# A mixer's tail folded into the next mixer's triangular inverse, in a two-layer hybrid trunk on one core

## The chip, the cores and the metric

The kernel runs on one core of one Trainium2 chip. The metric is the device time of one launch in microseconds (us). A profile is taken by the hardware on one execution; the span is the time from its first to its last instruction.

Names used below: TensorE (PE in the rows; PEld are its weight loads), VectorE (DVE), ScalarE (ACT), and SyncE (SP), whose queue issues every load of weights here. PSUM is a tile `ps` of eight banks of 128x512 float32.

## The reference

Two decoder layers over 256 tokens and 1024 channels. Each layer runs four mixers on 256 channels each, an output projection, a cross attention over 256 memory tokens and a feed-forward block (SwiGLU in layer 0, eight experts in layer 1).

```python
for l in range(DEPTH):
    h = rmsnorm(x, norm_mix[l]); p = h @ w_in[l]
    y_a = hgrn2_mixer(...)            # first mixer
    y_b = gated_deltanet_mixer(...)   # second mixer
    y_c = rglru_mixer(...)
    y_d = rwkv7_mixer(...)            # the mixer behind the second
    x = x + concat([y_a, y_b, y_c, y_d]) @ w_out[l]
    x = x + memory_cross_attention(rmsnorm(x), mem_n, wq, wk, wv, wo)
    x = x + (swiglu(...) if l % 2 == 0 else moe_swiglu(...))
```

The second mixer (gated DeltaNet) solves a unit triangular system for each chunk of 64 tokens and then steps a state:

```python
uw = triangular_solve(I + lower, rhs)          # lower: strict part of k k^T, decayed
v_new = u - w @ state
o = (q * exp(g)) @ state + scores @ v_new
state = exp(g_last) * state + k^T v_new
```

RWKV-7 is a recurrence of the same kind, and the kernel does it in the same chunked form, with a triangular inverse of its own. Keys and values of the memory (`mem_n @ wk`, `mem_n @ wv`) depend on nothing in the layer.

## The kernel before

Every engine has a program of its own, written out by hand; semaphores join them, and each engine runs its list strictly in the order of the code. In a layer the lists run: projection `w_in`, first mixer (`hgrn`), second mixer (`deltanet`), RWKV-7 (`rwkv`), output projection (`tm_part` and `tm_product` on `w_out`), attention, feed-forward.

**The inverses.** `inverse(i)` builds the inverse of a 64x64 unit triangular matrix for 8 pairs of head and chunk, by doubling, in levels v = 0 to 6 (`LEVELS` = 7) and two groups g. Inverse 2l belongs to DeltaNet and inverse 2l+1 to RWKV-7; I call them the first and the second inverse of layer l. A level goes around three engines: TensorE makes the products `inv_t`, VectorE masks them into `T1`, TensorE makes the products `inv_p`, then VectorE adds them to `X` while ScalarE copies `Y`. Behind each level TensorE calls `after(v)` and VectorE `beside(v)`: other work, written in between. The second inverse starts when VectorE has masked a score matrix into `N` (`mask(l, 0, ...)`, semaphore `inv_n`).

**DeltaNet's tail**, between the two inverses: `solve` for the first 128 tokens, a ScalarE copy, the state product, a VectorE mask of it (`state_bd`), the product `gd_km`, a VectorE subtraction (`gd_r1`), `solve` for the last 128 tokens, a copy, `outputs`, and the head norm (`head_ss`, then a logarithm and an exponential on ScalarE in `head_rms`, then `head_out` on VectorE). Each step waits for another engine.

**Filler.** The keys and values of the memory are made in eight pieces in a layer, `kv(l, i, ks)`: piece i is one chunk of weights, and each of its eight slices k is two float32 products. TensorE does slices of them wherever it would wait. `kv` waits first for the piece's load. I write kv6 for piece 6.

**Loads.** All chunks of weights (1024 KB each) go through three buffers `raw0` to `raw2`, in the order of `plan_chunks`, from one queue (SP). Load d waits until load d-3 is used up:

```python
if d >= RAW and loads[d - RAW][0] == "kv":
    sp.wait_ge(S("kv_done"), kv_load.index(d - RAW) + 1)
elif d >= RAW:
    sp.wait_ge(S("w_lo"), load_of.index(d - RAW) + 1)
```

A chunk that is not of the memory is used up when it is split into a high and a low part: `ahead(n)` on ScalarE makes `whi` from `raw`, `ahead(n)` on VectorE makes `wlo` (semaphore `w_lo`), each up to chunk n-1. Around the change the loads are, in layer 0: w_out 0, kv4, kv5, w_out 1, kv6, w_out 2, w_out 3, kv7; in layer 1: w_out 0, kv5, w_out 1, kv6, w_out 2, w_out 3, kv7. So w_out 1 and behind it kv6 (layer 0), and kv6 itself (layer 1), wait for the low part of w_out 0. TensorE needs kv6's first slices directly behind the second inverse.

## Time and profile before

| | |
|---|---|
| median of 3 runs | 1926.84 us (1923.26 to 1929.85) |
| profiled execution, its time | 1923.63 us |
| profiled execution, its span | 1921.8 us |
| TensorE busy | 1844.5 us (96% of the span) |
| VectorE busy | 1436.4 us (75%) |
| ScalarE busy | 1153.5 us (60%) |
| mean granted TensorE clock | 0.988 of full speed |

Busy time of TensorE counts the modelled ends of pipelined matmuls. In a row of the timeline the first number is the start, the second the length, `xN` the instructions merged, and the brackets give the idle time before and who ended it. One float32 product is two instructions in these rows.

### The profile page before, as it was taken

Reading aid. Unit: us, or ns where it says so; the run is one execution under the profiler, and the core shown is the slowest. Engines: PE = TensorE matmul, PEld = TensorE weight load, DVE = VectorE, ACT = ScalarE, POOL = GpSimd, SP = SyncE. Lnnn points to the kernel's source line nnn. Section 1 sums busy time; section 2 is a strip of 40 time slices with the busy share of each in tenths; the row PEclk is TensorE's granted clock in tenths of the full one; section 3 lists DMA queues with packets and bytes.
Section 4 is the critical chain, followed back from the end, with each engine's and each line's share of the span. In section 5 each row is a group of like instructions: output and inputs, shape, how many; then the busy total and the mean of one; then the engine's idle time right before and its main releaser. Section 6 shows DMA issues by size and latency. Waiting matters only on the chain.

```text
span 1921.8 us, 30255 instructions
## 1 busy us (share of the span) xinstructions
PE 1844.5 (96%) x12776; PEld 1589.5 (83%) x12777; DVE 1436.4 (75%) x1475; ACT 1153.5 (60%) x1129; POOL 0.2 (0%) x4
## 2 busy tenths in 40 slices
PE   7999999999999988996999999999999999999996
PEld 6988789999999877895788888888888888888884
DVE  6876654544458876545889989899898998989985
ACT  6565344434344653444677777677776777767774
POOL 0000000000000000000000000000000000000000
PEclk9999999999999999998999999999999999999998
DMA  7512224455555211234799999999999999999992
GB/s 247 162 60 68 68 88 168 164 189 181 176 173 172 66 46 68 88 132 167 288 365 368 361 333 377 350 370 365 326 386 341 365 372 332 382 364 340 371 374 87
DMA packets 239452, 466.02 MB, mean 242 GB/s; under 512 B 11856, under 2 KB 87760, under 8 KB 239312
## 3 DMA queue, kind: packets, MB, share of 16 engines
q1 hardware_dynamic: 239168, 463.93, 67.6%
q8 instruction: 103, 1.69, 0.4%
q14 instruction: 37, 0.30, 0.0%
q10 hardware_dynamic: 144, 0.11, 0.0%
HBM read 462.95 MB, written 1.05 MB: 241 GB/s over the span
## 4 chain that ended last, share of the span: by engine, by line
PE 92%; DVE 6%; issue 1%; ACT 1%; DVEq 0%; DMA 0%; ACTq 0%
PE ps L2265 32%; PE ps L1696 16%; PE ps L2275 16%; PE ps L1681 15%; PE ps L1716 8%; PE ps L2321 2%; PE ps L2296 1%; PE ps L1761 1%; DVE MT L974 1%; PE ps L2336 1%; DVE TMP L974 0%; DVE MT L977 0%; DVE hT_lo L980 0%; DVE MT L1216 0%; PE ps L1786 0%
## 5 line engine op out<-in xcount | busy, mean ns | idle before, releaser
L1458 DVE TENSOR_TENSOR wlo<-raw,whi 128x2048 fp32r<-128x2048 f32 x140 | 320.5, 2291 | 55.8 <-ACT whi L843 55.6
L843 ACT ACTIVATE whi<-raw 128x2048 fp32r<-128x2048 f32 x140 | 268.9, 1922 | 120.8 <-PE ps L2275 71.3
L987 DVE TENSOR_TENSOR wlo<-raw,whi 128x2048 fp32r<-128x2048 f32 x85 | 194.5, 2289 | 83.8 <-ACT whi L494 83.7
L1458 DVE TENSOR_TENSOR wlo<-PT,whi 128x2048 fp32r<-128x2048 f32 x84 | 192.1, 2292 | 31.2 <-ACT whi L843 30.2
L494 ACT ACTIVATE whi<-raw 128x2048 fp32r<-128x2048 f32 x85 | 162.2, 1908 | 80.1 <-PE ps L1716 31.9
L2265 PE MATMUL ps<-whi,hE_hi 128*128 128x512 f32 x672 | 185.4, 398 | 2.4 <-DVE hE_lo L1527 2.4
L843 ACT ACTIVATE whi<-PT 128x2048 fp32r<-128x2048 f32 x84 | 161.4, 1922 | 34.8 <-PE ps L2265 34.2
L2265 PE MATMUL ps<-wlo,hE_hi 128*128 128x512 f32 x672 | 180.1, 390 | 0.0
L2265 PE MATMUL ps<-whi,hE_lo 128*128 128x512 f32 x672 | 179.8, 389 | 0.0
L2265 PEld LDWEIGHTS ps<-wlo,hE_hi 128*128 128x128 f32 x672 | 126.2, 188 | 27.2
L2265 PEld LDWEIGHTS ps<-whi,hE_lo 128*128 128x128 f32 x672 | 126.1, 188 | 26.7
L2265 PEld LDWEIGHTS ps<-whi,hE_hi 128*128 128x128 f32 x672 | 122.0, 188 | 24.8 <-DVE hE_lo L1527 2.6
L2275 PE MATMUL ps<-whi,act_hi 128*128 128x512 f32 x336 | 130.8, 389 | 1.4 <-DVE act_lo L1502 1.4
L2275 PE MATMUL ps<-whi,act_lo 128*128 128x512 f32 x336 | 130.8, 389 | 0.0
L2275 PE MATMUL ps<-wlo,act_hi 128*128 128x512 f32 x336 | 130.7, 389 | 0.0
L1696 PE MATMUL ps<-hT_hi,whi 128*128 128x256 f32 x848 | 120.8, 285 | 0.0
L1696 PE MATMUL ps<-hT_hi,wlo 128*128 128x256 f32 x848 | 119.0, 283 | 0.0
L1696 PE MATMUL ps<-hT_lo,whi 128*128 128x256 f32 x848 | 119.0, 283 | 0.0
L1696 PEld LDWEIGHTS ps<-hT_hi,whi 128*128 128x128 f32 x848 | 110.1, 192 | 2.3 <-issue 1.4
L1696 PEld LDWEIGHTS ps<-hT_lo,whi 128*128 128x128 f32 x848 | 109.4, 192 | 0.0
L1696 PEld LDWEIGHTS ps<-hT_hi,wlo 128*128 128x128 f32 x848 | 109.4, 192 | 0.0
L485 ACT ACTIVATE MT<-ps 128x256 f32<-128x256 f32 (+2 forms) x94 | 43.9, 467 | 104.8 <-PE ps L1696 51.6
(301 smaller groups left out, 3337.8 us busy)
## 6 DMA issues: line engine op xcount, KB each, us to landing
raw<-in_moe_w_up SPq DMA_DIRECT2D x111, 1024.0 KB, 7.1
PT<-in_moe_w_down SPq DMA_DIRECT2D x56, 1024.0 KB, 6.7
PT<-in_moe_w_gate SPq DMA_DIRECT2D x55, 1024.0 KB, 7.0
TMP<-in_moe_w_gate SPq DMA_DIRECT2D x55, 1024.0 KB, 6.9
raw<-in_moe_w_down SPq DMA_DIRECT2D x55, 1024.0 KB, 5.9
raw<-in_w_in SPq DMA_DIRECT2D x28, 1024.0 KB, 5.5
raw<-in_ffn_w_gate SPq DMA_DIRECT2D x11, 1024.0 KB, 5.4
raw<-in_ffn_w_up SPq DMA_DIRECT2D x11, 1024.0 KB, 5.5
```

The lines of the kernel that those rows point to most:

```text
L485: return chain.link(lambda: nc.scalar.activation(o, i, f, **kw))
L494: nc.scalar.activation(whi[i % SPL][:, :], raw[d % RAW][:, :], ACT.Copy).then_inc(S("w_hi"), 1)
L843: nc.scalar.activation(ex_hi[m % XSPL], ex_raw[m % XRAW], ACT.Copy).then_inc(S("w_hi"), 1)
L974: return chain.link(lambda: V.tensor_tensor(o, x0, x1, op))
L987: V.tensor_tensor(wlo[i % SPL][:, :], raw[d % RAW][:, :], whi[i % SPL][:, :].bitcast(F32), ALU.subtract).then_inc(S("w_lo"), 1)
L1458: V.tensor_tensor(ex_lo[m % XSPL], ex_raw[m % XRAW], ex_hi[m % XSPL].bitcast(F32), ALU.subtract).then_inc(S("w_lo"), 1)
L1681: return Signalled(pe.matmul(o, lhsT, rhs, start=start, stop=stop, skip_group_check=True))
L1696: ins = pe.matmul(ps[:, bank, SEQ * m:SEQ * m + SEQ], wp[a_][:, k, P * m:P * m + P], src[b_][:, k, :], start=i == 0 and k == 0, stop=last)
L1716: ins = pe.matmul(ps[:, 4 + 2 * t + hf, :], src(b_, kk, t), wp[a_][:, kk, 512 * hf:512 * hf + 512], start=first and kk == 0 and i == 0, st ...
L2265: ins = pe.matmul(ps[:, bank, :], h_[b_][:, X_K * i + k, :], wp[a_][:, k, :], start=i == 0 and n_ == 0 and k == 0, stop=i == 1 and n_ == 2 ...
L2275: ins = pe.matmul(ps[:, 4 + hf, :], act_[b_][:, P * (TM_ROWS * i + kk):P * (TM_ROWS * i + kk) + P], wp[a_][:, kk, 512 * hf:512 * hf + 512] ...
L2321: ins = pe.matmul(g_tokens(c), xs[:, t, P * c:P * c + P], oneh[:, P * t:P * t + P], start=t == 0, stop=t == 1)
```

## The change

It touches both layers. DeltaNet's tail no longer stands between the inverses; its steps stand behind the levels of the second inverse, on all three engines. For that:

- The first RWKV score product, whose mask starts the second inverse, is made in `after(6)` of the first inverse, from operands that VectorE now finishes in `beside(5)` (`B_K`). Its mask is VectorE's next work after the first inverse.
- The second inverse's `Y` of levels 0 to 4 goes to a buffer of its own, since the tail still reads the first inverse's result. DeltaNet's output is copied to the other half of that buffer (`g_out`).
- The memory pieces that lay in the tail are dealt out over the levels again; slices 6 and 7 of kv5 come behind level 6.
- On VectorE, the split of w_out 0 (`ahead(first_chunk["w_out", l] + 1)`) moves from behind level 1's mask to behind the whole second inverse, and `head_out` stands behind it.
- On ScalarE, the high part of w_out 1 moves from level 5 into the RWKV tail, before the copy of the first `solve`. A wait for `head_out` stands ahead of it.

On ScalarE:

```diff
             def rwkv(l):
+                i = 2 * l + 1
+                inverse_turned(i)
+                inverse_first(i)
+                gdn_right(l, 0)
+                inverse_level(i, 1)
+                inverse_level(i, 2)
...
+                inverse_level(i, 3)
+                gdn_right(l, 1)
+                inverse_level(i, 4)
+                act.wait_ge(S("o_full"), 2 * l + 2)
+                a(tmp(6), ps[:, 6, :], ACT.Square)
+                a(g_out(l), ps[:, 6, :], ACT.Copy).then_inc(S("o_sq"), 1)
+                inverse_level(i, 5)
+                act.wait_ge(S("rk_kb"), 2 * l + 1)
+                act.wait_ge(S("o_ss"), 2 * l + 2)
+                a(tmp(7), ps[:, 6, :], ACT.Ln, scale=1.0 / HD, bias=epsc(0))
+                a(tmp(7), tmp(7), ACT.Exp, scale=-0.5).then_inc(S("o_rn"), 1)
...
                     if t == 0:
                         act.wait_ge(S("rk_trv"), 2 * l + 2)
                         a(tmp(6), ps[:, 3, :], ACT.Copy).then_inc(S("rk_vk"), 1)
+                        act.wait_ge(S("y_put"), 4 * l + 2)
+                        ahead(first_chunk["w_out", l] + 2)
                     act.wait_ge(S("rk_u"), 2 * l + t + 1)
                     a(tmp(4)[:, 256 * t:256 * t + 256], ps[:, 7, 256 * t:256 * t + 256], ACT.Copy, scale=-1.0).then_inc(S("rk_us"), 1)
```

On VectorE (`rk_kb` and `rk_ops` say that operands are ready):

```diff
                     tt(pt(B_Q), K_KA, K_EN, ALU.mult)
+                    tt(pt(B_K), K_KK, K_EM, ALU.mult).then_inc(S("rk_kb"), 1)
...
             def rwkv(l):
                 def beside(v):
 
                     if v == 0:
-                        head_out(l, 1, ps[:, 6, :], tmp(7), lambda c: pc("gdn_norm", l), pt(B_Z), 1)
+                        tt(pt(A_I), pt(D_R), K_E, ALU.mult).then_inc(S("rk_kb"), 1)
+                        tt(cm(pt(C_X))[:, :, 0:P], cm(K_KA)[:, :, 0:P], cm(pt(A_Q))[:, :, 0:P], ALU.mult)
+                        tt(cm(pt(C_X))[:, :, P:], cm(K_KK)[:, :, P:], cm(pt(A_F))[:, :, P:], ALU.mult)
                     if v == 1:
-                        ahead(first_chunk["w_out", l] + 1)
+                        dve.wait_ge(S("state"), 3 * l + 2)
...
                     if v == 2:
                         mask(l, 1, 4, mt(1), strict).then_inc(S("rk_m"), 1)
+                        dve.wait_ge(S("gd_km"), l + 1)
+                        tt(tmp(4)[:, 256:512], tmp(4)[:, 256:512], ps[:, 6, 256:512], ALU.subtract).then_inc(S("gd_r1"), 1)
+                    if v == 3:
+                        tt(cm(pt(B_V))[:, :, 0:P], cm(pt(D_K))[:, :, 0:P], cm(pt(A_Q))[:, :, 0:P], ALU.mult)
...
                         mask(l, 2, 4, PT[:, 0:1024], incl).then_inc(S("rk_m"), 1)
+                    if v == 5:
+                        tt(K_B, pt(D_R), pt(D_K), ALU.mult)
...
+                mask(l, 0, 4, mt(3), strict).then_inc(S("inv_n"), 1)
                 inverse(2 * l + 1, after=beside)
+                ahead(first_chunk["w_out", l] + 1)
+                head_out(l, 1, g_out(l), tmp(7), lambda c: pc("gdn_norm", l), pt(B_Z), 1)
...
                 rglru(l, LEVELS)
                 chain.settle()
                 ahead(first_chunk["w_out", l] + 2)
```

On TensorE; the first piece is in the first inverse's `after`, the rest in `rwkv`, the second's:

```diff
+                    if v == LEVELS - 1:
+                        pe.wait_ge(S("rk_kb"), 2 * l + 1)
+                        scores(4, pt(B_Q), pt(B_K)).then_inc(S("rk_sc"), 1)
...
             def rwkv(l):
+                k4 = ([0, 1, 2], [3, 4], [5, 6, 7], [], [], [], [])
+                k5 = ([], [], [], [0, 1, 2], [3, 4], [5], [6, 7]) if l == 0 else ([0], [1], [2], [3], [4], [5], [6, 7])
...
+                    kv(l, 5, k5[v])
                     if v == 0:
-                        kv(l, 4 + l, [6, 7])
...
+                        pe.wait_ge(S("rk_rn"), l + 1)
+                        solve(6, 0, tmp(4)).then_inc(S("gd_u"), 1)
...
+                        pe.wait_ge(S("gd_us"), 2 * l + 1)
...
                         scores(4, pt(A_G), pt(B_K)).then_inc(S("rk_sc"), 1)
+                    if v == 2:
+                        pe.wait_ge(S("state_bd"), 3 * l + 2)
...
                     if v == 3:
+                        pe.wait_ge(S("gd_r1"), l + 1)
+                        solve(6, 1, tmp(4)).then_inc(S("gd_u"), 1)
...
                         scores(4, pt(B_Q), pt(A_I)).then_inc(S("rk_sc"), 1)
+                    if v == 4:
+                        pe.wait_ge(S("gd_us"), 2 * l + 2)
+                        outputs(6, [(tmp(6), mt(2))], tmp(3)[:, 256:512], g_qe(l)).then_inc(S("o_full"), 1)
...
+                        head_ss(l, 1, tmp(6))
                     if v == LEVELS - 1:
-                        pe.wait_ge(S("y_put"), 4 * l + 2)
+                        pe.wait_ge(S("o_rn"), 2 * (l + 1))
...
                 inverse(2 * l + 1, after=turn_operands)
                 pe.wait_ge(S("rk_m"), 3 * (l + 1))
+                pe.wait_ge(S("rk_ops"), l + 1)
                 kv(l, 6, [0, 1])
```

**Where the split of w_out 0 stands.** This is VectorE in layer 0 before the change: levels 1 and 2 of the second inverse. `wlo2<-raw0` is the low part of w_out 0; L974 writes `T1` and `X`.

```order
L974 TENSOR_TENSOR MT<-ps,con16b 128x256 [waits y_put,inv_t]
L974 TENSOR_TENSOR MT<-ps,con16b 128x256 [waits inv_t1,inv_t]
L987 TENSOR_TENSOR wlo2<-raw0,whi2 128x2048 [waits w_hi]
L974 TENSOR_TENSOR MT<-MT,ps 128x256 [waits inv_t1,inv_p]
L974 TENSOR_TENSOR MT<-MT,ps 128x256 [waits inv_xy,inv_p]
L974 TENSOR_TENSOR MT<-ps,con16b 128x256 [waits inv_xy,inv_t]
L974 TENSOR_TENSOR MT<-ps,con16b 128x256 [waits inv_t1,inv_t]
```

With the change, the same engine at levels 5 and 6 and behind them; L1311 is the inverse's last copy.

```order
L986 TENSOR_SCALAR MT<-ps 64x256 [waits inv_xy,inv_t]
L986 TENSOR_SCALAR MT<-ps 64x256 [waits inv_t1,inv_t]
L989 SCALAR_TENSOR_TENSOR MT<-ps,con 128x1024 [waits inv_t1,rk_sc]
L1311 COPY MT<-ps 64x256 [waits rk_m,inv_p]
L1311 COPY MT<-ps 64x256 [waits inv_xy,inv_p]
L996 TENSOR_TENSOR wlo2<-raw0,whi2 128x2048 [waits w_hi]
L983 TENSOR_TENSOR TMP<-spare_hi1_50,TMP 128x512 [waits inv_xy,o_rn]
L989 SCALAR_TENSOR_TENSOR TMP<-TMP,par,PT 128x256 [waits dve_step] x2
```

The split has moved past five levels, to directly behind the last copy, with `head_out` behind it.

**The loads.** SP's list in layer 0 around them, the same rows in the same order in both kernels (the line numbers are those of the kernel with the change). `raw1<-in_xattn_wv`, second of the two, is kv6; the `raw0<-in_w_out` ahead of it is w_out 1.

```order
L437 DMA raw1<-in_xattn_wv 128x8x256 [waits kv_done]
L437 DMA raw2<-in_xattn_wv 128x8x256 [waits kv_done]
L437 DMA raw0<-in_w_out 128x2x1024 [waits w_lo]
L437 DMA raw1<-in_xattn_wv 128x8x256 [waits kv_done]
L437 DMA raw2<-in_w_out 128x2x1024 [waits kv_done]
```

No row moved: w_out 1 still waits for `w_lo`, the split of w_out 0, and kv6 still stands behind it.

**TensorE between the inverses.** Layer 0 before the change, from the last products of the first inverse to the tail's state product (`raw2` is the last filler of the first inverse, `raw1` is kv4).

```order
L1681 MATMUL ps<-MT 64x64 [waits inv_t1,inv_c]
L1681 MATMUL ps<-MT 64x64 x3
L1681 MATMUL ps<-memT_55,raw2 128x256 [waits raw_in2,kv_put]
L1681 MATMUL ps<-memT_55,raw2 128x256 x3
L1681 MATMUL ps<-TMP,MT 64x64 [waits rk_rn,inv_xy]
L1681 MATMUL ps<-TMP,MT 64x64 x7
L1681 MATMUL ps<-raw1,memT_55 128x256 [waits raw_in1,kv_put]
L1681 MATMUL ps<-raw1,memT_55 128x256
L1681 MATMUL ps<-TMP 128x128 [waits gd_us]
L1681 MATMUL ps<-TMP 128x128
```

The same place with the change:

```order
L1689 MATMUL ps<-MT 64x64 [waits inv_t1,inv_c]
L1689 MATMUL ps<-MT 64x64 x3
L1689 MATMUL ps<-memT_55,raw2 128x256 [waits raw_in2,kv_put]
L1689 MATMUL ps<-memT_55,raw2 128x256 x3
L1689 MATMUL ps<-PT 128x128 [waits rk_kb]
L1689 MATMUL ps<-PT 128x128 x7
L1689 MATMUL ps<-MT,con 64x64 [waits inv_n,inv_xy]
L1689 MATMUL ps<-MT,con 64x64 x15
L1689 MATMUL ps<-con,spare_hi1_50 64x64 [waits inv_c,inv_xy]
```

The score product (`PT`, waits `rk_kb`) has come forward to the filler's end, and the second inverse's first product, which waits for `inv_n`, stands directly behind it with no filler between them.

**TensorE at the end of the second inverse**, layer 0 with the change; `raw1` is kv6, `raw2` kv5.

```order
L1689 MATMUL ps<-MT 64x64 [waits inv_t1,inv_c]
L1689 MATMUL ps<-MT 64x64 x3
L1689 MATMUL ps<-raw2,memT_55 128x256 [waits raw_in2,raw_in1]
L1689 MATMUL ps<-raw2,memT_55 128x256 x3
L1692 MATMUL ps<-con,PT 128x128 [waits o_rn]
L1692 MATMUL ps<-con,PT 128x128 x3
L1689 MATMUL ps<-raw1,memT_55 128x256 [waits rk_ops,raw_in1,rk_m,inv_xy]
L1689 MATMUL ps<-raw1,memT_55 128x256 x3
L1689 MATMUL ps<-TMP,MT 128x64 [waits rk_vk]
L1689 MATMUL ps<-TMP,MT 128x64 x3
```

Before it was the same without the two `raw2` rows: slices 6 and 7 of kv5 have come behind level 6, and kv6's first slices still follow the four transposes.

## Rows read from the trace of the kernel before

**Rows 1.** The page, part 4: the chain that ended last, by engine.

```profile
PE 92%; DVE 6%; issue 1%; ACT 1%; DVEq 0%; DMA 0%; ACTq 0%
```

**Rows 2.** Windows: length; busy PE, PEld, DVE, ACT, POOL; PEclk; DMA; GB/s.

```profile
186.20:233.70 47.50, 44.45 (x800) 36.80 (x800) 26.45 (x49) 14.91 (x26) 0.00 (x0) 1.00 0.25 82
235.30:239.00 3.70, 3.68 (x10) 2.94 (x11) 3.46 (x6) 0.29 (x1) 0.00 (x0) 0.54 0.01 2
725.70:766.20 40.50, 36.68 (x768) 31.26 (x767) 26.41 (x49) 14.91 (x26) 0.00 (x0) 1.00 0.22 80
767.90:771.40 3.50, 3.50 (x9) 2.79 (x10) 3.32 (x6) 0.00 (x0) 0.00 (x0) 0.51 0.00 0
```

**Rows 3.** Timeline of TensorE, layer 0, from the first inverse on.

```profile
184.29 1.99 PE L1681 MATMUL ps<-memT,raw 128*128 128x256 f32 x8
...
195.55 1.16 PE L1681 MATMUL ps<-PT 64*128 64x128 f32 x16
...
199.42 1.15 PE L1681 MATMUL ps<-MT,con 64*64 64x64 f32 x32
...
212.97 1.22 PE L1681 MATMUL ps<-MT 64*64 64x64 f32 x64 [0.15 <-DVE MT L974]
...
231.22 2.46 PE L1681 MATMUL ps<-MT 64*64 64x64 f32 x32
233.62 0.66 PE L1684 MATMUL ps<-con,PT 128*128 128x128 f32 x4
235.32 3.63 PE L1681 MATMUL ps<-raw,memT 128*128 128x256 f32 x8 [1.04 <-DVE MT L1301]
```

**Rows 4.** Timeline of VectorE, layer 0, same stretch.

```profile
189.04 0.42 DVE L974 TENSOR_TENSOR TMP<-ps,con 128x256 f32<-128x256 f32 x1 [4.23 <-PE ps L1681]
...
196.75 1.23 DVE L980 SCALAR_TENSOR_TENSOR MT<-ps,con 128x1024 f32<-128x1024 f32 x1 [1.19 <-PE ps L1681]
198.01 0.87 DVE L974 TENSOR_TENSOR MT<-MT,con16b 64x256 f32<-64x256 f32 x2
198.92 0.43 DVE L974 TENSOR_TENSOR MT<-ident_b,MT 128x256 f32<-128x256 f32 x1
...
206.60 2.28 DVE L987 TENSOR_TENSOR wlo<-raw,whi 128x2048 fp32r<-128x2048 f32 x1
...
234.32 0.94 DVE L1301 COPY MT<-ps 64x256 f32<-64x256 f32 x2
```

**Rows 5.** Timeline of SP's queue, layer 0: w_out 1, then kv6.

```profile
208.91 0.37 SPq L431 DMA_DIRECT2D raw<-in_w_out  x1
209.32 0.47 SPq L431 DMA_DIRECT2D raw<-in_xattn_wv  x1
```

**Rows 6.** Issues of that stretch: KB each, us from issue to landing.

```profile
raw<-in_w_out SPq DMA_DIRECT2D x1, 1024.0 KB, 4.8
raw<-in_xattn_wv SPq DMA_DIRECT2D x1, 1024.0 KB, 7.4
```

**Rows 7.** Timeline of TensorE, layer 1.

```profile
763.77 2.46 PE L1681 MATMUL ps<-MT 64*64 64x64 f32 x32
...
767.86 3.68 PE L1681 MATMUL ps<-raw,memT 128*128 128x256 f32 x8 [1.04 <-DVE MT L1301]
```

**Rows 8.** Timeline of VectorE, layer 1.

```profile
766.87 0.94 DVE L1301 COPY MT<-ps 64x256 f32<-64x256 f32 x2
```

**Rows 9.** Issue of kv6 in layer 1, at 748.37.

```profile
raw<-in_xattn_wv SPq DMA_DIRECT2D x1, 1024.0 KB, 5.2
```

**Rows 10.** Issues at 288.7 to 290, three behind each other.

```profile
raw<-in_xattn_wo SPq DMA_DIRECT2D x1, 1024.0 KB, 10.8
```

**Rows 11.** Timeline of ScalarE, layer 0.

```profile
229.48 1.91 ACT L494 ACTIVATE whi<-raw 128x2048 fp32r<-128x2048 f32 x1
...
242.39 0.38 ACT L485 ACTIVATE TMP<-ps 128x256 f32<-128x256 f32 x1 [1.45 <-PE ps L1681]
```

**Rows 12.** A window early in the span, columns as in rows 2.

```profile
26.80:31.40 4.60, 4.55 (x26) 3.02 (x27) 3.01 (x10) 0.00 (x0) 0.00 (x0) 0.63 0.87 258
```

More of the change, by code:

```diff
@@ L1276, in inverse @@
                 N, X, Y, T1 = mt(3), X_INV, mt(5), mt(0)
+                Y0 = y_work(i)
                 for v in range(LEVELS):
@@ L1368, in deltanet @@
                 inverse(2 * l, after=beside)
-                dve.wait_ge(S("state"), 3 * l + 2)
-                tt(tmp(3)[:, 256:512].rearrange("p (c n) -> p c n", c=2), ps[:, 1, 0:256].rearrange("p (c n) -> p c n", c=2),
-                   rep(bdones, 2), ALU.mult).then_inc(S("state_bd"), 1)
-                dve.wait_ge(S("gd_km"), l + 1)
-                tt(tmp(4)[:, 256:512], tmp(4)[:, 256:512], ps[:, 1, 256:512], ALU.subtract).then_inc(S("gd_r1"), 1)
-                rwkv_operands(l)
-                mask(l, 0, 2, mt(3), strict).then_inc(S("inv_n"), 1)
             def rwkv(l):
@@ L1386, in beside @@
+                    if v == 3:
+                        tt(cm(pt(B_V))[:, :, 0:P], cm(pt(D_K))[:, :, 0:P], cm(pt(A_Q))[:, :, 0:P], ALU.mult)
+                        tt(cm(pt(B_V))[:, :, P:], cm(pt(D_R))[:, :, P:], cm(pt(A_Q))[:, :, P:], ALU.mult)
                     if v == 4:
                         mask(l, 2, 4, PT[:, 0:1024], incl).then_inc(S("rk_m"), 1)
+                    if v == 5:
+                        tt(K_B, pt(D_R), pt(D_K), ALU.mult)
+                        for c in range(2):
+                            s_ = slice(256 * c, 256 * c + 256)
+                            ts(K_B[:, s_], K_B[:, s_], pc("rwkv_r_k", l, c), ALU.mult).then_inc(S("rk_ops"), 1 if c else 0)
@@ L2081, in deltanet @@
-                for c in range(2):
-                    mm(ps[:, 1, P * c:P * c + P], tmp(3)[:, P * c:P * c + P], tmp(6)[:, P * c:P * c + P]).then_inc(S("state"), 1 if c else 0)
-                kv(l, 4 + l, [1])
-                pe.wait_ge(S("state_bd"), 3 * l + 2)
-                for c in range(2):
-                    mm(ps[:, 1, 256 + P * c:256 + P * c + P], g_kbe(l)[:, 256 * c + P:256 * c + 256], tmp(3)[:, 256 + P * c:256 + P * c + P]).then_inc(S("gd_km"), 1 if c else 0)
-                kv(l, 4 + l, [2])
@@ L2088, in deltanet @@
-                pe.wait_ge(S("gd_r1"), l + 1)
-                solve(6, 1, tmp(4)).then_inc(S("gd_u"), 1)
-                kv(l, 4 + l, [3])
-                pe.wait_ge(S("gd_us"), 2 * l + 2)
-                outputs(6, [(tmp(6), mt(2))], tmp(3)[:, 256:512], g_qe(l)).then_inc(S("o_full"), 1)
-                pe.wait_ge(S("rk_kb"), l + 1)
-                scores(2, pt(B_Q), pt(B_K)).then_inc(S("rk_sc"), 1)
-                head_ss(l, 1, tmp(6))
-                kv(l, 4 + l, [4, 5])
             def rwkv(l):
+                k4 = ([0, 1, 2], [3, 4], [5, 6, 7], [], [], [], [])
@@ L2107, in turn_operands @@
                     if v == 1:
-                        pe.wait_ge(S("rk_ops"), l + 1)
-                        pe.wait_ge(S("o_rn"), 2 * (l + 1))
+                        pe.wait_ge(S("gd_us"), 2 * l + 1)
+                        for c in range(2):
+                            mm(ps[:, 6, P * c:P * c + P], tmp(3)[:, P * c:P * c + P], tmp(6)[:, P * c:P * c + P]).then_inc(S("state"), 1 if c else 0)
                         scores(4, pt(A_G), pt(B_K)).then_inc(S("rk_sc"), 1)
+                    if v == 2:
+                        pe.wait_ge(S("state_bd"), 3 * l + 2)
+                        for c in range(2):
+                            mm(ps[:, 6, 256 + P * c:256 + P * c + P], g_kbe(l)[:, 256 * c + P:256 * c + 256], tmp(3)[:, 256 + P * c:256 + P * c + P]).then_inc(S("gd_km"), 1 if c else 0)
@@ L2143, in rwkv @@
                 pe.wait_ge(S("rk_rs"), 2 * l + 1)
-                solve(7, 0, tmp(7)).then_inc(S("rk_u"), 1)
+                solve(7, 0, tmp(2)).then_inc(S("rk_u"), 1)
                 kv(l, 6, [3])
@@ L2155, in rwkv @@
                 pe.wait_ge(S("rk_rs"), 2 * l + 2)
-                solve(7, 1, tmp(7)).then_inc(S("rk_u"), 1)
+                solve(7, 1, tmp(2)).then_inc(S("rk_u"), 1)
                 kv(l, 6, [6])
```

81 lines of the change are left out of this document (29 added, 52 removed).

## The prediction

> **What bounds the kernel now.** I read the chain that ended last first: 92% of it is TensorE, 6% VectorE [rows 1]. So an edit pays where it takes an idle time of TensorE away, and costs where it puts one in. Then I took the two stretches that the change rebuilds, from the last filler of the first inverse to the last products of the second (levels 0 to 6). In layer 0 TensorE is busy for 44.45 of 47.50 us, in layer 1 for 36.68 of 40.50 [rows 2]. That leaves 3.05 and 3.82 us of idle time, and no more can be won inside them: the products themselves stay the same. The reader is to see how little this is. DeltaNet's tail looks like a serial chain (solve, copy, product, mask, solve), and VectorE does wait in it, 4.23 us ahead of the state mask [rows 4]; but TensorE fills the waits with slices of the memory's keys and values.
>
> Last, what stands behind the second inverse. There TensorE waits 1.04 us for VectorE's last copies, in both layers, and then does kv6's first two slices in 3.63 and 3.68 us [rows 3, 7], where two slices took 1.99 us at the end of the first inverse [rows 3]. The granted clock is the reason: 0.54 and 0.51 in these stretches against 1.00 before them [rows 2], so most of them ran at 1.2 instead of 2.4 GHz. That costs 1.7 us a layer, and it is paid already.
>
> The question that decides is whether kv6's load has landed when TensorE comes to it. In layer 0 it is issued at 209.32 and takes 7.4 us, so it lies ready at 216.7, 18 us before its use at 235.32 [rows 3, 5, 6]. In layer 1 it is issued at 748.37 and takes 5.2 us, 14 us before 767.86 [rows 7, 9]. Both issues follow the low part of w_out 0 at once (206.60 plus 2.28 is 208.88, and w_out 1 goes out at 208.91 [rows 4, 5]). The change puts that split behind the second inverse.
>
> **The change, part by part.** Let Z be the end of the second inverse's last products on TensorE: before 231.22 + 2.46 = 233.68 in layer 0, 763.77 + 2.46 = 766.23 in layer 1 [rows 3, 7]. First how far Z moves, then what happens behind it.
>
> Taken out ahead of Z: the old idle time, 3.05 and 3.82 us, and two slices of kv5 that now come behind level 6, 1.9 us by the row at 184.29 less the 0.07 by which it overlaps the next [rows 3]. All other TensorE work (solve, state, outputs, scores, slices) only changes places.
>
> Put in ahead of Z, in each layer:
> - The score product is now the last thing before VectorE's mask, and the second inverse's first product stands right behind the mask with no filler between. TensorE waits for the whole mask, 1.23 us plus two handoffs of 0.04 (the score product ends at 196.71, the mask starts at 196.75 [rows 3, 4]): 1.3 us.
> - The start of the inverse. VectorE makes `Y` of one group in 0.87 + 0.43 us [rows 4], of both in 2.6. TensorE has 1.15 us of its own transposes [rows 3] and then group 0's. Waits between 0.2 (1.3 against 1.15) and 1.5 us (2.6 against 1.15); I take 0.6, near the low end, since group 0's transposes lie in it. Before, ScalarE's head norm stood in this place and TensorE had slices.
> - Five levels with 0.15 us each between `inv_t` and `inv_p`, as before [rows 3]: 0.75 us.
> - Level 1: VectorE waits for the state product before it adds to `X`; the level's score product on TensorE covers it. I take 0.1.
> - Level 2: `gd_km` is TensorE's last product of the level. Behind it come VectorE's subtraction and then its addition to `X`, both of 128x256 as the row of 0.42 us [rows 4], with three handoffs, and TensorE has nothing left: 1.1 us. Queued behind that subtraction on VectorE is the rest of the inverse. Bounds 0.9 and 1.3.
> - `B_K` in level 5 of the first inverse: 128x512, some 0.8 us at twice that row, mostly under a filler of 1.9 us: 0.2, bounds 0 and 0.8.
>
> Together 4.05 us. Z moves by -3.05 - 1.9 + 4.05 = -0.9 us in layer 0 and by -3.82 - 1.9 + 4.05 = -1.7 us in layer 1. So the overlap wins almost nothing: it changes filler that covered waits for waits that the tail's steps cover.
>
> Behind Z. VectorE's last copies end 1.6 us behind Z (234.32 + 0.94 = 235.26; 766.87 + 0.94 = 767.81 [rows 4, 8]). The mask of level 6 is ahead of them as before, so I keep 1.6. Then comes the split of w_out 0, 2.3 us [rows 4]. Only then can SP issue: in layer 0 w_out 1, 0.4 us later kv6, which lands 7.4 us on [rows 5, 6]; in layer 1 kv6 at once, landing after 5.2 us [rows 9]. So kv6 is there at Z + 1.6 + 2.3 + 0.4 + 7.4 = Z + 11.7 in layer 0 and at Z + 1.6 + 2.3 + 5.2 = Z + 9.1 in layer 1. TensorE is through with its two slices and the transposes (0.6 us [rows 3]) at Z + 2.5. It stands still for 9.2 and 6.6 us, and everything of the RWKV tail is queued behind kv6's slices on TensorE.
>
> Before, kv6 began at Z + 1.6. The loss is -0.9 + 11.7 - 1.6 = 9.2 us in layer 0 and -1.7 + 9.1 - 1.6 = 5.8 us in layer 1, together 15.0 us.
>
> For this landing the Trainium skill, "DMA: Bandwidth & Descriptors", "Anatomy of one DMA", has a fit: some 2.0 us fixed and the rest at 436 GB/s. By that a chunk of 1 MB would take 4.4 us and two behind each other 6.8, an estimate; the rows have 5.2 and 7.4, and with the page's figures the loss would be 1.4 us less. The page measured another issuing path, and the row decides. The sum needs neither sentence.
>
> At no cost I take: the clock (the slices behind the wait start at the low clock before and, I expect, after; bounds below); ScalarE's new copy and the head norm (ScalarE is busy for 14.91 of 47.50 us there [rows 2]); the high part of w_out 1, 1.91 us ahead of the copy of the first solve. ScalarE idled 1.45 us there [rows 11], so the copy comes 0.5 us late, and one slice of kv6 (1.0 us) stands on TensorE between the solve and the use. Without that slice it would cost 0.5 a layer. VectorE's scans and w_out 1's low part come later too, under the RWKV tail; its list is nearly empty there.
>
> The sum is made against the profiled execution: 1923.63 + 15.0 = 1938.6. The median of the runs is 1926.84, 3.2 above it; I carry the change over to it: 1941.8, rounded to 1942.
>
> **The rivals.**
>
> *kv6 is not waited for, and the kernel gets faster* (0.06). It would take a landing by Z + 2.5, that is an issue 6.6 us earlier in layer 1 and 9.2 in layer 0, from a split that I misplace. Then kv6 starts 0.9 us later behind Z than before: -0.9 + 0.9 = 0 in layer 0, -0.8 in layer 1. The 1.04 us for the copies is gone into that, and with the gap filled the clock may stay up, 1.7 us a layer. Together -4.2: 1922.6. For it speaks that the copies and the low clock are real costs; against it the two rows that tie the issue to the split.
>
> *The wait comes but most of it is won back* (0.08). TensorE's delay also gives the other engines time, and if a later stage were bound by loads alone, it would give that back. It decides from 9 us on (within 5.8 us, or 0.3%, of before). But the loads of the attention wait for splits that stand in the same lists behind the RWKV tail, so they move with it. Time 1927 to 1932.
>
> *The clock and the loads make it worse* (0.10). After the wait TensorE starts at the low clock; in an early window the granted clock is 0.63 over 4.6 us [rows 12], the same 1.7 us of loss as behind the second inverse. If the fall lasts twice as long in the denser tail, 1.7 us more in each layer. And w_out 2 is now issued directly behind kv6 in layer 0; with three loads behind each other the last took 10.8 us [rows 10], against 7.4: 3.4 us more in layer 0. All of it gives 15 + 3.4 + 3.4 = 21.8: 1948.6, and with the 0.5 us copies 1950.
>
> *Forecast* (0.76): 1942, its own span 1936 to 1948.
>
> **How the numbers follow.** About 0.3% (5.8 us) is what a measurement of this kernel can tell from no change. Low end: a landing in layer 0 of 4.8 instead of 7.4 us (-2.6) [rows 6] and the low bounds of the waits (0.4 + 0.2 + 0.2 a layer, -1.6), against the profiled execution's own base: 1923.6 + 10.8 = 1934.4. High end: the third rival, 1950. Range 1934 to 1950; it leaves out the first two rivals and little of the third. Faster 0.06, same 0.08, slower 0.86.
>
> **What would show it.** In the profile after: SP's issue of kv6 2.3 us behind VectorE's last copies of the second inverse (2.7 in layer 0), the low part of w_out 0 directly between them; idle times of TensorE of some 9 and 6.5 us ahead of kv6's first slices, put down to a load; those slices at a granted clock near 0.5; 1.3 us of idle ahead of the second inverse for the mask, 1.1 in its level 2; the stretch up to Z shorter by 1 to 2 us. It is wrong if kv6 is issued well before the inverse ends, if its load lands in half the time, or if the stretch up to Z grows or shrinks by several microseconds, which a wait that I have not seen in the new interleaving would do.

## The result, and the profile after

The changed kernel takes 1943.14 us (median of 4 runs, 1942.95 to 1946.9), the kernel before 1925.62 us in the same comparison (4 runs, 1923.26 to 1929.85). The ratio is 1.0094, with a 95% interval from 1.0077 to 1.0111: slower by 17.5 us. The profiled execution took 1943.08 us with a span of 1941.2, against 1923.63 and 1921.8: 19.4 us more.

The chain that ended last, from the page of the kernel after (to [rows 1]); a load is on it now:

```profile
PE 90%; DVE 7%; DMA 1%; issue 1%; ACT 1%; DVEq 0%; SPq 0%; ACTq 0%
```

The timeline of TensorE in the kernel after, layer 0, answers to [rows 3]; L1689 is the old L1681.

```profile
183.75 1.99 PE L1689 MATMUL ps<-memT,raw 128*128 128x256 f32 x8
...
188.25 1.15 PE L1689 MATMUL ps<-MT,con 64*64 64x64 f32 x32 [1.42 <-DVE MT L989]
...
192.79 4.88 PE L1689 MATMUL ps<-raw,memT 128*128 128x256 f32 x12
...
208.03 2.86 PE L1689 MATMUL ps<-raw,memT 128*128 128x256 f32 x12
...
212.36 1.21 PE L1689 MATMUL ps<-MT 64*64 64x64 f32 x32 [1.04 <-DVE MT L983]
...
232.11 2.47 PE L1689 MATMUL ps<-MT 64*64 64x64 f32 x32
234.51 1.99 PE L1689 MATMUL ps<-raw,memT 128*128 128x256 f32 x8
236.34 0.60 PE L1692 MATMUL ps<-con,PT 128*128 128x128 f32 x4
246.82 3.75 PE L1689 MATMUL ps<-raw,memT 128*128 128x256 f32 x8 [9.88 <-DMA raw<-in_xattn_wv]
250.36 1.56 PE L1689 MATMUL ps<-TMP,MT 128*128 128x64 f32 x8
```

The 9.88 us are the new thing: TensorE stands still until kv6 has landed. Why it lands so late stands on VectorE and in SP's queue. First VectorE's timeline in the kernel after, behind the last products of the second inverse (it answers to [rows 4]):

```profile
235.22 0.93 DVE L1311 COPY MT<-ps 64x256 f32<-64x256 f32 x2
236.08 2.27 DVE L996 TENSOR_TENSOR wlo<-raw,whi 128x2048 fp32r<-128x2048 f32 x1
238.28 0.68 DVE L983 TENSOR_TENSOR TMP<-spare_hi,TMP 128x512 f32<-128x512 f32 x1
```

and SP's queue in the same kernel (to [rows 5]), in both layers:

```profile
238.38 0.37 SPq L437 DMA_DIRECT2D raw<-in_w_out  x1
238.79 0.47 SPq L437 DMA_DIRECT2D raw<-in_xattn_wv  x1
...
781.43 0.37 SPq L437 DMA_DIRECT2D raw<-in_xattn_wv  x1
```

The issues of kv6 in the kernel after, KB and us from issue to landing, first layer 0, then layer 1 (to [rows 6, 9]):

```profile
raw<-in_xattn_wv SPq DMA_DIRECT2D x1, 1024.0 KB, 7.9
raw<-in_xattn_wv SPq DMA_DIRECT2D x1, 1024.0 KB, 5.5
```

238.79 + 7.9 is 246.7, and TensorE starts at 246.82. Layer 1 has the same picture in TensorE's timeline (to [rows 7]): Z is 775.16 + 2.47 = 777.63, and 781.43 + 5.5 is 786.9.

```profile
775.16 2.47 PE L1689 MATMUL ps<-MT 64*64 64x64 f32 x32
...
787.02 3.75 PE L1689 MATMUL ps<-raw,memT 128*128 128x256 f32 x8 [7.04 <-DMA raw<-in_xattn_wv]
```

Last the clock, in windows of the kernel after (columns as in [rows 2]):

```profile
190.00:197.00 7.00, 7.00 (x51) 6.05 (x49) 2.35 (x5) 1.19 (x2) 0.00 (x0) 0.51 0.04 11
197.00:234.00 37.00, 35.26 (x678) 29.43 (x678) 14.98 (x32) 8.86 (x19) 0.00 (x0) 1.00 0.01 2
236.90:241.70 4.80, 0.04 (x1) 0.00 (x0) 4.14 (x6) 2.48 (x3) 0.00 (x0) 0.96 0.43 137
241.70:251.00 9.30, 4.18 (x12) 3.50 (x12) 0.00 (x0) 0.00 (x0) 0.00 (x0) 0.50 0.73 268
251.00:262.00 11.00, 11.00 (x88) 9.37 (x89) 5.26 (x8) 3.82 (x6) 0.00 (x0) 0.98 0.01 1
```

It fell to the lower level (1.2 GHz) during the wait for kv6 and stayed there for its first slices, as expected. But it also fell at the start of the second inverse in layer 0, some 2 us behind the short wait for the mask (0.51 from 190.00 to 197.00): the 12 products at 192.79 took 4.88 us where 12 such products take 2.86 (208.03).

**The balance.** I cut each execution at the first product of `w_out` in each layer. All columns are from TensorE's timelines; "to Z'" runs from the last slices of the first inverse (183.75 above) to the start of the second inverse's last products (232.11 above).

| us, profiled execution | layer 0: slices to Z' | layer 0: slices to w_out | from there to w_out of layer 1 | from there to the end |
|---|---|---|---|---|
| before | 46.93 | 69.11 | 532.55 | 1135.85 |
| after | 48.36 | 81.74 | 539.78 | 1135.93 |
| split back in level 1 | 48.39 | 69.35 | 532.86 | 1137.88 |
| late split alone | 46.34 | 79.95 | 542.52 | 1140.39 |
| split in level 0 | 45.52 | 66.48 | 530.50 | 1140.48 |
| mask's wait filled | 44.66 | 65.61 | 529.47 | 1137.69 |
| gd_km first | 43.55 | 64.51 | 528.82 | 1135.94 |
| and ScalarE's high part back | 43.55 | 64.51 | 529.45 | 1136.03 |
| kv6 later on TensorE | 45.52 | 76.91 | 539.49 | 1136.04 |
| kv6 and ScalarE's part later | 48.36 | 75.72 | 536.29 | 1137.84 |
| before, filled behind its inverse | 45.54 | 66.50 | 530.92 | 1136.15 |

The rows stand for single executions. Those of "before, filled behind its inverse", "kv6 later on TensorE", "gd_km first" and "kv6 and ScalarE's part later" lie 4.3, 4.7, 3.9 and 3.7 us under the medians of their kernels, so the table compares stages, and the medians below compare kernels.

After against before: +12.63 in layer 0 and +7.23 up to layer 1's `w_out`. Of the latter, 6.53 lie behind the last slices of layer 1's first inverse (68.73 against 62.20 us) and 0.70 ahead of them. With +0.08 behind and -0.54 ahead of the table this makes the span's 19.4.

### The profile page after: what moved, and what is told of

Same layout as the page of the kernel before. It is cut to its first block, busy times and chain, and to the rows that moved or that the text cites. A ratio compares the mean times of both kernels' runs of the same rounds, so it can differ in the third digit from the quotient of the medians.

```text
span 1941.2 us, 30264 instructions
## 1 busy us (share of the span) xinstructions
PE 1847.5 (95%) x12776; PEld 1592.7 (82%) x12777; DVE 1436.2 (74%) x1475; ACT 1153.8 (59%) x1131; POOL 0.2 (0%) x4
## 4 chain that ended last, share of the span: by engine, by line
PE 90%; DVE 7%; DMA 1%; issue 1%; ACT 1%; DVEq 0%; SPq 0%; ACTq 0%
PE ps L2275 32%; PE ps L2285 16%; PE ps L1704 15%; PE ps L1689 14%; PE ps L1724 8%; PE ps L2331 2%; PE ps L2306 1%; DVE MT L983 1%; PE ps L1769 1%; PE ps L2346 1%; DMA raw<-in_xattn_wv 1%; DVE wlo L996 1%; DVE TMP L983 0%; DVE MT L986 0%; DVE hT_lo L989 0%
## 5 line engine op out<-in xcount | busy, mean ns | idle before, releaser
L1689 PEld LDWEIGHTS ps<-MT 64*64 64x64 f32 (+1 forms) x1856 | 58.6, 137 | 34.3 <-DVE MT L983 21.6
```

The source lines that it names most:

```text
L1689: return Signalled(pe.matmul(o, lhsT, rhs, start=start, stop=stop, skip_group_check=True))
```

## The experiments

My theory at this point: the late split of w_out 0, which holds back kv6's load, makes nearly all of the loss. Its rival: the interleaving of the tail with the inverse costs by itself.

**The split back in level 1.**

```diff
                     if v == 1:
+                        ahead(first_chunk["w_out", l] + 1)
                         dve.wait_ge(S("state"), 3 * l + 2)
...
                 inverse(2 * l + 1, after=beside)
-                ahead(first_chunk["w_out", l] + 1)
```

> The changed kernel with one thing undone: the split of the first output weight chunk stands again in level 1 of the second inverse, ahead of the wait for the state product, and not behind the inverse. Theory (the late split makes memory piece 6 late, and everything else of the change costs 2 us or less): piece 6 is issued in the first half of the second inverse, has landed long before Z, TensorE starts its slices 1.6 to 2.5 us after Z in both layers, the 12.2 and 9.4 us of the changed kernel are gone, and so is the low clock behind them; 1924 to 1929 us, 14 to 19 us under the change. The fall of the clock at the start of the second inverse in layer 0 stays (12 small slices in 4.9 us). Rival A (the interleaving itself costs: its waits for the mask, for level 2, the longer level 0): the time stays at 1936 us or above, and piece 6 starts early without the end moving. Rival B (the split, 2.3 us on VectorE ahead of the masked state, delays level 2 on TensorE, which the change wanted free of it): TensorE waits 2 us or more for VectorE at level 2 in each layer, 1929 to 1933 us.

Measured: 1926.72 us (1919.58 to 1930.07, 12 runs), ratio to before 1.0006 [0.9993, 1.002]. All of the loss is gone with this one line, within the interval, whose upper end is 0.2%. TensorE's timeline behind Z in this kernel, layer 0 (Z is 235.26), has no wait, and the slices run at the full clock: they took 3.63 us before.

```profile
232.80 2.46 PE L1689 MATMUL ps<-MT 64*64 64x64 f32 x32
235.20 1.99 PE L1689 MATMUL ps<-raw,memT 128*128 128x256 f32 x8
237.03 0.60 PE L1692 MATMUL ps<-con,PT 128*128 128x128 f32 x4
237.47 1.89 PE L1689 MATMUL ps<-raw,memT 128*128 128x256 f32 x8
```

The rival's 1936 us is out. TensorE's wait at level 2 stayed at 1.04 us, so the split did not delay it (my second rival). The fall of the clock at the inverse's start is in this execution too: its stretch to Z' is 48.39 us.

**The late split alone, in the kernel before.**

```diff
-                    if v == 1:
-                        ahead(first_chunk["w_out", l] + 1)
...
                 inverse(2 * l + 1, after=beside)
+                ahead(first_chunk["w_out", l] + 1)
                 rglru(l, LEVELS)
```

> The kernel before with one part of the change alone: the split of the first output weight chunk is moved from level 1 of the second inverse to behind it, ahead of the first step of the RG-LRU part. Nothing of the interleaving is in it. Theory: piece 6 is issued about 3.2 us behind the last copies of the inverse and lands 5.2 to 8 us later, so TensorE starts its slices at Z + 12 in layer 0 and Z + 9.2 in layer 1 where it was Z + 1.6; 10.5 + 7.6 us, and about 0.6 us for the low clock behind the wait: 1942 to 1946 us, the time of the whole change. Rival (what costs is the interleaving, and the wait for piece 6 is one that some other late work would have filled anyway): 1926 to 1932 us.

Measured: 1947.97 us (1940.41 to 1948.7, 6 runs), ratio 1.0105 [1.0086, 1.0124]; the whole change had 1.0094. One moved instruction, repeated in two layers, makes the whole loss by itself. TensorE's timeline in it, layer 0 and layer 1:

```profile
230.08 2.47 PE L1680 MATMUL ps<-MT 64*64 64x64 f32 x32
244.62 3.75 PE L1680 MATMUL ps<-raw,memT 128*128 128x256 f32 x8 [11.48 <-DMA raw<-in_xattn_wv]
...
775.34 2.47 PE L1680 MATMUL ps<-MT 64*64 64x64 f32 x32
786.97 3.75 PE L1680 MATMUL ps<-raw,memT 128*128 128x256 f32 x8 [8.57 <-DMA raw<-in_xattn_wv]
```

kv6 starts 12.07 us behind Z in layer 0 and 9.16 in layer 1, the expected 12 and 9.2. The time is 2 us above the expected range.

**The split in level 0**, where VectorE is idle.

```diff
                     if v == 0:
...
+                        ahead(first_chunk["w_out", l] + 1)
```

> As the first kernel of this call, but the split stands at the end of VectorE's steps of level 0 of the second inverse, where VectorE idles 7.1 us in layer 0 and 2.5 us in layer 1 in the changed kernel. Theory: it hides there whole (2.27 us) in layer 0 and nearly so in layer 1, so level 2's wait of 1.04 us is not lengthened; the time is that of the first kernel or up to 2 us under it, 1922 to 1928 us. Rival (the split delays the state's mask or level 1's products in layer 1, where the gap is just its length): layer 1 is 1 to 2 us longer there than in the first kernel.

Measured: 1924.4 us (12 runs), ratio 0.9992 [0.998, 1.0003]. As expected, but against the first experiment the intervals overlap, so the place within the first levels is not shown to matter. Its rival, 1 to 2 us more in layer 1, did not come: the stretch from the last slices to Z' is 39.01 us there, 0.40 more than in the first experiment. By the time, the interleaving with the split out of its way is worth nothing that 12 runs can tell. The balance does show its two stages 2.63 and 2.05 us shorter than before's, and its last 1136 us, which the change does not touch, 4.63 us longer. The last experiment says where the shorter stages come from.

**The mask's wait filled.**

```diff
                 inverse(2 * l, after=rwkv_ahead)
+                pe.wait_ge(S("kv_put"), 2 * NH * l + 4 + l)
+                kv(l, 4 + l, [0])
...
-                k4 = ([0, 1, 2], [3, 4], [5, 6, 7], [], [], [], [])
+                k4 = ([1, 2], [3, 4], [5, 6, 7], [], [], [], [])
```

(and `[0]` out of `k5` in layer 1).

> As the third kernel of this call, and one slice of the memory piece that follows (eight matmuls of about 0.25 us at full clock, some 0.95 to 2 us in all) stands between the score product and the second inverse on TensorE, taken out of level 0's list, so that TensorE has work while VectorE makes the mask (1.42 us of waiting in each layer of the changed kernel). Theory: the wait is filled in both layers, 1.0 to 1.4 us less in each; and if it was this pause that let the clock fall in layer 0, the clock stays up at the inverse's start there and 2.3 us more come back: 2.0 to 5 us under the third kernel, 1919 to 1924 us. Rival (the slices only move from one place to another, since level 0 has to wait for ScalarE's turned copies either way, so the wait comes back at level 0 or 1): within 0.7 us of the third kernel. Rival for the clock: it falls in layer 0 all the same, as it is the run of 64 by 64 products ahead of the mask and not the pause that lowers it.

Measured: 1920.9 us (1918.28 to 1924.46, 12 runs), ratio 0.9977 [0.9965, 0.9988]: faster than before, and 3.5 us under the third experiment by the medians. Both had 12 runs on one chip; their means differ by 3.3 us, with a 95% interval of about 1.9 to 4.7. By the balance the two stages are 0.87 and 1.03 us shorter. Its timeline of TensorE, layer 0:

```profile
186.75 1.13 PE L1689 MATMUL ps<-raw,memT 128*128 128x256 f32 x4
188.15 1.15 PE L1689 MATMUL ps<-MT,con 64*64 64x64 f32 x32 [0.27 <-DVE MT L989]
```

The 1.42 us are 0.27. The clock stayed up at the inverse's start in this profile; whether the fill did that is not shown, since it also stayed up in other executions without it (below).

**gd_km ahead of the slices**, on top of that.

```diff
                 def turn_operands(v):
+                    if v == 2:
+                        pe.wait_ge(S("state_bd"), 3 * l + 2)
...
                     if l == 0:
                         kv(0, 4, k4[v])
```

(the whole branch with the two `gd_km` products, moved up from below the slices).

> The kernel with the slice that fills the mask's wait (split in level 0), and one thing more: at level 2 of the second inverse the two products of the first mixer that VectorE waits for (gd_km) stand on TensorE ahead of the slices of the memory piece and not behind them. In the kernel of before this edit VectorE idles 2.77 us in layer 0 for them (203.65 plus 1.23, then 207.64) and TensorE then waits 1.04 us for VectorE at the next level, in both layers. Theory (that wait is a chain TensorE slices, gd_km, VectorE, TensorE): VectorE is done while TensorE makes its slices, the two waits of 1.04 us go, 2.1 us less than the kernel it is built on, 1918 to 1919.5 us. Rival (the wait just turns up at a later level, since VectorE's steps are what bounds the inverse): within 0.5 us of 1920.9.

Measured: 1918.82 us (1914.92 to 1919.52, 5 runs), ratio 0.9967 [0.9954, 0.998], in the middle of the expected range. The waits of TensorE for VectorE's tile in the window 185 to 262, first with the mask's wait filled, then in this kernel (us in total, times, longest):

```profile
PE ps L1689 <- DVE MT L983: 1.3, 3, 1.0
```

```profile
PE ps L1689 <- DVE MT L983: 0.5, 3, 0.2
```

The intervals of the two kernels overlap, and they were measured on different chips, each beside its own runs of before (the ratios differ by 0.001, 1.9 us). So the 2.1 us rest on these waits and on the balance (1.10 us in layer 0, 0.65 behind it).

**ScalarE's high part of w_out 1 back** behind level 5, on top of that.

```diff
                 a(tmp(7), tmp(7), ACT.Exp, scale=-0.5).then_inc(S("o_rn"), 1)
+                ahead(first_chunk["w_out", l] + 2)
...
-                        act.wait_ge(S("y_put"), 4 * l + 2)
-                        ahead(first_chunk["w_out", l] + 2)
```

> The first kernel of this call with ScalarE's high part of output weight chunk 1 put back near its old place: behind level 5 of the second inverse and the exponent for the head norm, without the wait for the last of the layer's y, where the change had put it between the two right sides. Theory (its place costs nothing, as the next weight loads are early enough either way): within 0.7 us of the kernel it is built on. Rival (the loads behind it come 7 us later than in the kernel before and push later chunks, or the 1.9 us on ScalarE between the copies of the right sides and the solves lengthens that chain): 1 to 2.5 us less.

Measured: 1918.57 us (5 runs), ratio 0.9961 [0.9949, 0.9974]: the same as the kernel it is built on, as far as five runs tell. Its new place costs nothing that they show. This and the one before are the fastest kernels of the study, some 7 us under before.

**kv6 later on TensorE**, the split still late.

```diff
-                kv(l, 6, [0, 1])
...
-                kv(l, 6, [2])
...
-                kv(l, 6, [3])
...
-                kv(l, 6, [4])
...
                 right_side(1)
-                kv(l, 6, [5])
+                kv(l, 6, [0])
...
-                kv(l, 6, [6])
+                kv(l, 6, [1])
...
-                kv(l, 6, [7])
+                kv(l, 6, range(2, KT))
```

> The changed kernel, its late split untouched, with the slices of memory piece 6 moved on TensorE: none stands ahead of the first right side, of the first solve, of the state product or of the second right side; slice 0 stands behind the second right side, slice 1 behind the second solve, the other six behind the outputs. Theory (what costs is that everything of the second mixer's solve is queued on TensorE behind slices whose weights have not landed): piece 6 is issued and lands as late as before, at Z + 9.4 and Z + 12.2, but the steps ahead of it (some 7 to 8 us of products with waits for ScalarE and VectorE between them) run meanwhile; 4 to 6 us are won in each layer, less what the six slices behind the outputs cost nothing for: 1931 to 1936 us. Rival (the load is late for something else than these slices too, the split that VectorE owes to piece 6's buffers or a queue behind it): 1940 us or more, with the wait only in another place.

Measured: 1942.61 us (1937.73 to 1949.9, 6 runs), ratio 1.0098 [1.0079, 1.0116]. The theory missed and its rival holds: the load wait of TensorE is gone, the time is not, and a wait stands in another place. TensorE's timeline in this kernel and, under it, ScalarE's, layer 0:

```profile
237.17 1.25 PE L1689 MATMUL ps<-TMP,MT 64*64 64x64 f32 x16 [0.87 <-ACT TMP L491]
243.08 2.07 PE L1689 MATMUL ps<-TMP 128*128 128x128 f32 x8 [4.65 <-ACT TMP L491]
```

```profile
240.84 1.91 ACT L500 ACTIVATE whi<-raw 128x2048 fp32r<-128x2048 f32 x1 [3.13 <-DMA raw<-in_w_out]
242.66 0.37 ACT L491 ACTIVATE TMP<-ps 128x256 f32<-128x256 f32 x1
```

The late split makes two loads late. w_out 1 is the other, and ScalarE has its high part queued ahead of the copy that the state product needs. In the changed kernel this stood hidden behind the wait for kv6.

**And ScalarE's part later too.**

```diff
-                        act.wait_ge(S("y_put"), 4 * l + 2)
-                        ahead(first_chunk["w_out", l] + 2)
...
+                act.wait_ge(S("y_put"), 4 * l + 2)
+                ahead(first_chunk["w_out", l] + 2)
                 act.wait_ge(S("rk_o"), l + 1)
```

> The kernel with memory piece 6 moved behind the second right side (split still late), and one thing more: ScalarE's high part of output weight chunk 1, for which it waits until that chunk has landed, stands behind its last copy for the solves and no longer between the copies of the first right side and of the first solve. In the kernel it is built on, ScalarE waits 3.13 us for that load in layer 0 (240.84, then 1.91 us for the high part), and TensorE waits 4.65 us for ScalarE's copy behind it (243.08), and 2.09 us in layer 1. Theory (the late split makes two loads late and the second mixer's solve stands behind both: on TensorE behind piece 6, on ScalarE behind the output chunk): with both taken out of the way the waits of 4.65 and 2.09 us shrink to about 0.8 us each, and the clock does not fall for them, which gives 2 us more back; 1933 to 1938 us, 5 to 9 us under the 1942.6 of the kernel it is built on. Rival A (the time is bound by piece 6's landing alone, so TensorE now waits for it ahead of slice 0, 4 us or more): 1940 us or above. Rival B (its high part is now late for VectorE's split and TensorE's output product): a wait of 2 us or more ahead of the third output chunk's products, 1938 us or above.

Measured: 1939.75 us (1936.04 to 1946.55, 6 runs), ratio 1.0079 [1.0062, 1.0097]. Half a miss. TensorE's timeline:

```profile
242.33 1.16 PE L1689 MATMUL ps<-TMP 128*128 128x128 f32 x8 [0.47 <-ACT TMP L491]
...
246.97 1.13 PE L1689 MATMUL ps<-raw,memT 128*128 128x256 f32 x4 [1.41 <-DMA raw<-in_xattn_wv]
```

The 4.65 us fell to 0.47 as expected (in layer 1 the 2.09 also to 0.47), and 1.41 us of waiting for the load came in. By the balance the two stages are 1.19 and 3.20 us shorter than in the kernel it is built on, and this execution had the clock's fall at the inverse's start, 2.84 us, which that one had not. The medians differ by 2.9 us only, and the intervals overlap. That both waits hang on the late split is shown by the rows; the size of this repair is not. Neither rival came as written: the wait for the load was 1.41 us, not 4, and no wait for a chunk stands ahead of the products of `w_out`.

Nor is this kernel repaired: it is still 13.5 us above before. From Z' to `w_out` it takes 6.40 us more in layer 0 and 3.24 in layer 1 than the kernel with the split in level 0, whose TensorE waits for nothing there. Of these, 4.0 and 2.6 us are waits in the RWKV solve, 2.1 us a layer for ScalarE's copies alone. The slices of kv6 covered them before they were moved away.

**The kernel before, filled behind its inverse** (layer 0 alone).

```diff
-                    if l == 0 and 1 <= v < 6:
+                    if l == 0 and 1 <= v < 7:
...
-                        kv(0, 5, ([0], [1, 2], [3], [4, 5], [6, 7])[v - 1])
+                        kv(0, 5, ([0], [1, 2], [3], [4], [5], [6, 7])[v - 1])
```

> The kernel before, with one thing of the change: in layer 0 the last slices of memory piece 5 do not stand ahead of the last level's products but behind them, as the changed kernel has them in both layers (slices [0], [1, 2], [3], [4], [5] in levels 1 to 5, [6, 7] behind the last products; before they ended with level 5). Nothing else is changed, layer 1 not at all. It asks whether what the mended kernels win behind Z (slices 0 and 1 of piece 6 in 1.9 us, with no wait ahead of them, where the kernel before waits 1.04 us and takes 3.6 us for them at half the clock) is owed to this filling. Theory: in layer 0 the wait of 1.04 us goes and the clock stays up, 1.7 us for the slices and 0.5 us for what follows, less up to 1 us of waiting at the last levels where a slice is now missing: 1922 to 1924 us against 1924.6. Rival (the clock falls there all the same, from the 32 products of 64 columns ahead, which run at 2.46 us where they should take 1.2): 1924 to 1925 us.

Measured: 1923.88 us (12 runs) against 1925.83, ratio 0.9997 [0.9988, 1.0007]: by the time alone, no change. Its profile has what was expected, in TensorE's timeline:

```profile
229.77 2.46 PE L1681 MATMUL ps<-MT 64*64 64x64 f32 x32
232.16 1.99 PE L1681 MATMUL ps<-raw,memT 128*128 128x256 f32 x8
234.00 0.60 PE L1684 MATMUL ps<-con,PT 128*128 128x128 f32 x4
234.43 1.89 PE L1681 MATMUL ps<-raw,memT 128*128 128x256 f32 x8
```

No wait of 1.04 us, and kv6's slices in 1.89 us instead of 3.63; the stage is 2.61 us shorter. At 66.50 us it is as long as that of the kernel with the split in level 0 (66.48). So in layer 0 what the mended kernels win comes from slices placed behind Z, not from the tail's interleaving. My rival blamed the 2.46 us of the last products on the clock; the granted clock over them is 1.00.

Of the two parts of this win only the wait is tied to the slices in every profile. TensorE's timeline of the same kernel in layer 1, which this edit does not touch, shows the wait with the clock up:

```profile
765.25 1.99 PE L1681 MATMUL ps<-raw,memT 128*128 128x256 f32 x8 [1.04 <-DVE MT L1301]
```

The kernel before has 3.68 us in this place. So the 1.7 us of low clock come in some executions and not in others, and the table's column up to layer 1's `w_out` is 1.63 us shorter here without any edit in it.

That the whole time doesn't show the 2.61 us is left open. The interval's lower end is 2.3 us under before, and executions scatter by more than that, as told at the end.

## Why the prediction was right

**The mechanism.** Every step of it stands in the trace: the split directly behind VectorE's last copies, SP's issues at its end, a wait for a load of 9.88 and 7.04 us (predicted 9.2 and 6.6), the first slices behind it at half the clock. The second experiment shows that the moved split alone makes the time of the change, the first that nothing else in the change costs more than 0.2%.

**Behind Z.** kv6 starts at Z + 12.24 and Z + 9.39 (11.7 and 9.1). The differences are the landings: 7.9 and 5.5 us for the 7.4 and 5.2 that I carried over.

**Ahead of Z.** The mask's wait was 1.42 (1.3), level 2's 1.04 (1.1). Z moved by -1.39 us in layer 1 (-1.7). In layer 0 it moved by +1.44 where I had -0.9. This is the term that failed: I put the clock "at no cost" and looked for its fall only behind the wait. It fell behind the new wait for the mask as well. The kernel with kv6 later on TensorE has the same code up to Z and did not fall there: its stretch is 45.52 us against 48.36, so the fall cost 2.84 us, and without it Z moved by -1.4. The other terms of the sum can be read from windows over the same stretches (columns as in [rows 2]): first that kernel's layer 0, then layer 1 of the kernel after.

```profile
185.59:231.64 46.05, 42.54 (x792) 35.91 (x791) 20.84 (x42) 11.98 (x25) 0.00 (x0) 1.00 0.08 25
```

```profile
738.47:777.63 39.16, 35.65 (x760) 29.84 (x759) 20.85 (x42) 11.38 (x24) 0.00 (x0) 1.00 0.09 29
```

TensorE is idle for 3.51 us in each, where I had 3.85 (4.05 less the 0.2 for `B_K`, which lies ahead of the stretch). The start of the inverse waited 0.2 us at most and not 0.6, and of the five waits of 0.15 us two are left. The two slices of kv5 took 1.9 us off the busy time in layer 0 (44.45 to 42.54), as I had it, but in layer 1 only 1.03 us went (36.68 to 35.65); why is open.

**The sum.** 12.0 and 6.4 us (9.2 and 5.8), and 0.8 us of low clock in the slices and the right sides, 19.2 of the span's 19.4. Of the 4.2 us that the sum lacked, 2.3 lie ahead of Z in layer 0, where the clock fell (+1.44 for -0.9), 0.3 ahead of Z in layer 1, 0.8 in the landings and 0.8 in that low clock behind them. Predicted were 15.0. The median was nonetheless met within 1.2 us, and that is partly luck: I carried the sum over from the profiled execution to a median of three runs, 3.2 us higher, and so made up for most of a sum that was 4.4 us short of the profiled difference. Against the medians' difference of 17.5 us it was 2.5 short. With more runs the median of before was 1924.6 (29 runs), 1925.8 (17) and 1926.3 (11).

**What I gave too little weight.** I named a high part of w_out 1 that comes 0.5 us late on ScalarE. That it also waits for its own late load I did not say. In the changed kernel it cost nothing, and it became 4.65 us as soon as kv6 was out of the way.

**The rivals.** That kv6 is in time was wrong. Of its other half, that a filled gap behind Z keeps the clock up and gives 1.7 us a layer, the profiles bear out this much: with slices in the gap and kv6 in time the clock stayed up in all eleven places of six kernels, without them it fell in two of three. Nothing was won back later: behind layer 1's `w_out` the two kernels take 1135.85 and 1135.93 us. The third rival's dearer landing of three loads did not come for kv6, the second of them (7.9 us); the third, w_out 2, took 9.9 us, and TensorE waited for nothing there. Its longer fall of the clock, 1.7 us a layer, was 0.6 and 0.2 us; the clock's dear fall was the one ahead of Z, which no rival had.

## What to carry to other kernels

An instruction that frees a buffer is part of the load chain, though it takes 2.3 us on an engine with idle time: ask of each such step that is moved which loads wait for it, on which engines those loads are awaited, and what is queued there. When a repair takes away one wait, look for a second consumer of the same late event before pricing it. A slice moved out of the way of a late load also leaves the wait that it covered. The interleaving, which replaces covered waits by other covered waits, won nothing by itself here; the gains came from memory slices behind the inverse and in the mask's wait, and from two products put ahead of slices.
